# All bias tables first, x loaded after slot 3, DVE's root and scaled tiles before the last four conditioning additions, the sixth conditioning total behind norm 1's sums

## The chip, the cores and the metric

The kernel runs on one core of one Trainium2 chip. The metric is the device time of that core in microseconds (us). The trace is one profiled execution. Engines: PE (TensorE), ACT (ScalarE), DVE (VectorE), POOL (GpSimd), SP (SyncE, which here only issues loads).

## What is computed

Two transformer blocks on x of 256 tokens by 1024, then a norm. What the change touches is the first block's entrance and its second norm:

```python
cond = jax.nn.silu(c)
mod = (cond @ w_ada[l] + b_ada[l]).reshape(b, 6, d)
shift1, scale1, gate1, shift2, scale2, gate2 = [mod[:, i] for i in range(6)]
hn = modulate(rmsnorm(x, norm1_g[l]), shift1, scale1)     # modulate: h * (1 + scale) + shift
proj = hn @ w_in[l]                                       # w_qi is one part of w_in
ya = dsa_attention(..., rel_bias)                         # adds rel_bias by distance of query and key
...
x = x + gate1[:, None, :] * (merged @ w_out[l])           # w_out is w_o in the kernel
hn2 = modulate(rmsnorm(x, norm2_g[l]), shift2, scale2)
f = peer_ffn(hn2, peer_wq[l], ...)                        # w_pq in the kernel
```

## The kernel before

x stands transposed in xT (128 rows by 8 tiles of 256 tokens). Every weight comes as tiles of 128 by 1024 floats (512 KB), in one fixed order (`stream_plan`): 16 tiles of the conditioning weights w_ada, then w_qi (4), w_ki, w_wi, w_qb and so on. Between later tiles the other 32 of w_ada are strewn. Each tile has a slot; the first weights use seven in turn, slots 0 to 3 in `ringb` and 4 to 6 in `far`. SP issues the loads in this order, and waits before each until the slot's last tile has been used up. ACT turns a weight tile into its rounded high part (L1266), DVE (L1794) or POOL (L2574) computes the low part, and PE multiplies with three matmuls for each product (`mm3`).

Conditioning tiles go another way: DVE multiplies each with a column of cond = silu(c) and adds it to `ada_acc` (`ada_add`, L1828 for the first of eight, L1831 for the others). After eight of them PE sums over the rows with eight matmuls of one column (`ada_total`; the trace counts 16, as each float matmul goes in two passes), and DVE adds b_ada (`mod_part`, L1810). The six parts come in the order scale1, shift1, gate1, shift2, scale2, gate2; part g is finished when `mod_done` is g. The scale of part 1 stays in a PSUM bank and goes into the column sm[:, 24:32] (L1996, L1998).

Each engine has a program of its own, written out in order, and waits on semaphores only where it says so. There is no planner; the order in the code is the order of execution. The first stretch:

- ACT: loads vecs, oh and rel_bias, makes cond, waits for slot 5's first tile, issues the loads of cst (identity and ones) and xT, loads the table of the root (L1424), copies bias tables 0 to 3 from PSUM to `sg` (L1428), squares the eight tiles of xT (L1315, with rows of rT used in turn, so that the fifth square waits for the first sum), does the root (L1346), copies bias tables 4 to 7, and then the high parts of the first weights (`splits`).
- PE: bias tables 0 to 3 (`bias_tables`: one matmul of 32 rows and 384 columns for each head, once POOL has spread rel_bias, L2611), sums the squares (`sum_up`, eight matmuls), the first conditioning total, bias tables 4 to 7, the second total, and then the matmuls of w_qi on H.
- DVE: additions of all 16 tiles, the root's correction (L1858 to L1862), the scale column, the eight scaled tiles of x (`scaled`, L1974), mod part 2, and the low parts of H (L2005), each after ACT's high part (L1356).
- POOL: the eight replications, the low parts of w_qi's first two tiles, and then the transfers of the bias tables through DRAM that skew them by rows (L2618, L2623). Before these it waits for the landing of w_qi's fourth tile.

Around the second norm (norm 1 in the code): PE does w_pb, w_pa, the sixth total, w_o, and then the sums of norm 1's squares (`total(1)`). DVE merges the branches in `w_pa`'s loop (L2119 to L2123, the last of which is the low part of H), does mod part 6, waits for mod_done 6, makes the scale column for norm 1 (L2126, L2128), and adds w_o's results to xT (L1904), with low parts of the weights between.

Of the kernel before, what the change touches and what calls it, by code (L numbers as in the profile page):

```python
# [73 lines left out]
def flat(ap):  # L74
    return ap.rearrange("p a b -> p (a b)")
# [226 lines left out]
def square_row(q, k):  # L302

    return ROW[k % 4] if q in (0, 3) or k == 0 else (3, 4, 0)[(k - 1) % 3]


def adds_before(q):
    return sum(ADDS[:q])
# [6 lines left out]
def scaled_before(q):  # L315

    return q - (q > 4)
# [38 lines left out]
def build(nc, A, out, scratch, x_kept):  # L356
    with ExitStack() as ctx:
        V, S, G, TE, SP = nc.vector, nc.scalar, nc.gpsimd, nc.tensor, nc.sync
        P = stream_plan()
# [7 lines left out]
        def sem(name):  # L367
            return ctx.enter_context(nc.semaphore(name))
# [114 lines left out]
        def vec(name, j, n=1):  # L483
            o = VO[name] + j
            return vecs[:, o:o + n]


        slot_in = [sem(f"slot_in{i}") for i in range(13)]
# [6 lines left out]
        cond_done, ada_done, ada_sum, mod_done, mod_prep = (sem(n) for n in ("cond_done", "ada_done", "ada_sum", "mod_done", "mod_prep"))  # L495
# [34 lines left out]
        def ada_bank(g):  # L530

            return 3 if g == 1 else 6
# [17 lines left out]
        def recip(q):  # L550

            return banks[2][:, T:2 * T] if q == 3 else rT[:, 0, :] if q == 4 else banks[7][:, T:2 * T]
# [39 lines left out]
        def tensor_program(t):  # L592
# [4 lines left out]
            def mm(o, l, r, start, stop):  # L597
                return TE.matmul(o, l, r, start=start, stop=stop, skip_group_check=True)  # L598
# [6 lines left out]
            def claim(b):  # L605
                if freed[b]:
                    t.wait_ge(*freed[b])
                return banks[b]

            def ada_total():  # L610
                g, pending = divmod(st["ada"], 8)
                if pending or g == st["sum"]:
                    return
                st["sum"] = g
                b = ada_bank(g - 1)
                o = claim(b)
                t.wait_ge(ada_done, 8 * g)
                t.wait_ge(cst_in, 16)
                for j in range(8):
                    last = mm(o[:, j:j + 1], ada_acc[:, (g - 1) % 2, j * 128:(j + 1) * 128], ones[:, 0:1], True, True)  # L620
                last.then_inc(ada_sum, 1)
                freed[b] = (mod_done, g)

            def ada_unit():
                ada_total()
                st["pos"] += 1
                st["ada"] += 1
# [86 lines left out]
            def of(X):  # L714
                return lambda k: (X[:, 0, k, :], X[:, 1, k, :])
# [9 lines left out]
            def sum_up(q, src, first, last):  # L725
                mm(banks[7][:, 0:T], ones, src, first, last).then_inc(sq_sum, 1)

            def total(q):

                claim(7)  # L730
                t.wait_ge(cst_in, 16)
                t.wait_ge(sq_add, adds_before(q) + 5)
                sum_up(q, squares_sum, True, False)
                for k in (6, 7):
                    t.wait_ge(sq_done, 8 * q + k + 1)
                    sum_up(q, rT[:, square_row(q, k), :], False, k == 7)
                freed[7] = (r_done, q + 1) if q in (4, 6) else (n_t, 8 * scaled_before(q) + 8)
# [83 lines left out]
            def bias_tables(heads):  # L821
                for h in heads:
                    o = claim(bias_bank[h])
                    t.wait_ge(oh_in, 16)
                    t.wait_ge(b_rep, h + 1)
                    mm(o[:, 0:384], ohs[:, 512 + 128 * h:640 + 128 * h], ohs[:, 0:384], True, True).then_inc(b_mm, 1)
                    freed[bias_bank[h]] = (b_cp, h + 1)

            bias_tables(range(4))
            claim(7)  # L830
            t.wait_ge(cst_in, 16)
            for k in range(8):
                t.wait_ge(sq_done, k + 1)
                sum_up(0, rT[:, square_row(0, k), :], k == 0, k == 7)
            freed[7] = (n_t, 8)
            for _ in range(8):
                ada_unit()
            ada_total()
            bias_tables(range(4, 8))
            for _ in range(8):  # L840
                ada_unit()
            ada_total()
# [100 lines left out]
            while U[st["pos"]][0] == "w_ada":  # L943
                ada_unit()
            lin("w_pa", 8, of(Ya), lambda k: t.wait_ge(a_yl, k + 1), kt=4)
            ada_total()
            lin("w_o", 8, hk, lambda k: t.wait_ge(mg_lo, k // 2 + 1))
            total(1)


            def key_scores(c):
# [301 lines left out]
        def scalar_program(s):  # L1253
# [79 lines left out]
            def root(q):  # L1333
                if q == 3:
                    s.wait_ge(s2_sum, 8)
                    s.wait_ge(c_eps, 2)
                    S.activation(s2, banks[3][:, 0:T], ACT.Identity, bias=eps2).then_inc(s2_cp, 1)
                    s.wait_ge(r_done, q)
                    s.wait_ge(z_done, 1)
                    S.activation(rT[:, 1, :], mean(q), ACT.Abs_reciprocal_sqrt).then_inc(rt_done, 1)  # L1340
                    return
                s.wait_ge(sq_sum, sums_before(q + 1))
                s.wait_ge(c_eps, 1)
                if q:
                    s.wait_ge(r_done, q)
                S.activation(rT[:, 1, :], mean(q), ACT.Abs_reciprocal_sqrt, bias=eps).then_inc(rt_done, 1)  # L1346
# [70 lines left out]
            S.dma_start(ohs[:, 384:392], A["rel_bias"]).then_inc(rb_in, 16)  # L1417
            s.wait_ge(vecs_in, 16)
            S.activation(cond[:, :], vec("c", 0, 8), ACT.Silu).then_inc(cond_done, 1)
            s.wait_ge(slot_in[P.slot[5]], 16 * P.use[5])  # L1420
            S.dma_start(cst[:, :], A["cst"]).then_inc(cst_in, 16)
            S.dma_start(xT[:, :, :], A["xT"]).then_inc(x_in, 16)
            s.wait_ge(c_eps, 1)
# [1 line left out]
            def bias_tables(heads):  # L1425
                for h in heads:
                    s.wait_ge(b_mm, h + 1)
                    S.copy(sg[:, 384 * h:384 * h + 384], banks[bias_bank[h]][:, 0:384]).then_inc(b_cp, 1)  # L1428

            bias_tables(range(4))  # L1430
            s.wait_ge(x_in, 16)
            for k in range(8):
                square(0, k, xT[:, k, :])
            root(0)
            bias_tables(range(4, 8))
            for _ in range(16):
                splits()
            s.wait_ge(mod_done, 2)
# [345 lines left out]
        def vector_program(v):  # L1784
# [12 lines left out]
            def lows():  # L1797
                st["pos"] += 1
                lows_until(st["pos"])
# [5 lines left out]
            def mod_part(g):  # L1805
                st["sum"] = g
                o, c = banks[ada_bank(g - 1)], 8 * PARTS[g - 1]
                v.wait_ge(ada_sum, g)
                v.wait_ge(vecs_in, 16)
                V.tensor_tensor(mod[:, c:c + 8], o[:, 0:8], vec("b_ada", c, 8), ALU.add).then_inc(mod_done, 1)  # L1810

            def ada_total():
                g, pending = divmod(st["ada"], 8)
                if not pending and g != st["sum"]:
                    mod_part(g)

            def ada_add():
                n = st["pos"]
                g, k = divmod(st["ada"], 8)
                st["ada"] += 1  # L1820
                lows()
                acc, w = ada_acc[:, g % 2, :], slots[P.slot[n]]
                v.wait_ge(slot_in[P.slot[n]], 16 * P.use[n])
                if k == 0:
                    v.wait_ge(cond_done, 1)
                    if g >= 2:
                        v.wait_ge(ada_sum, g - 1)
                    V.tensor_scalar(acc, w, cond[:, 0:1], None, ALU.mult).then_inc(ada_done, 1)  # L1828
                else:
                    v.wait_ge(ada_done, P.raw_no[n] - 1)  # L1830
                    V.scalar_tensor_tensor(out=acc, in0=w, scalar=cond[:, k:k + 1], in1=acc, op0=ALU.mult, op1=ALU.add).then_inc(ada_done, 1)  # L1831

            def ada_unit():
                ada_total()
                ada_add()
# [46 lines left out]
            def norm(*a, **k):  # L1882
                for _ in norm_steps(*a, **k):
                    pass
# [87 lines left out]
            def scaled(tiles):  # L1972
                for j in tiles:
                    V.scalar_tensor_tensor(out=xs3[:, j, :], in0=xT[:, j, :], scalar=sm[:, 24 + j:25 + j], in1=recip(0),  # L1974
                                           op0=ALU.mult, op1=ALU.mult).then_inc(n_t, 1)
# [10 lines left out]
            V.scalar_tensor_tensor(out=gfm, in0=vec("final_g", 0, 8), scalar=-2.0, in1=vec("norm_mix_g", 0, 8), op0=ALU.mult, op1=ALU.mult).then_inc(c_half, 1)  # L1986
            b1 = vec("b_ada", 8, 8)
            V.tensor_scalar(b1, b1, 1.0, None, ALU.add).then_inc(mod_prep, 1)
            for _ in range(1, 16):
                ada_add()  # L1990
            root(0)

# [5 lines left out]
            V.tensor_tensor(sm[:, 24:32], o[:, 8:16], vec("norm1_g", 0, 8), ALU.mult).then_inc(mod_done, 1)  # L1998
            v.wait_ge(mod_done, 1)
            scaled(range(8))  # L2000
            mod_part(2)
            v.wait_ge(mod_done, 2)
            for j in range(8):
# [111 lines left out]
            for c in range(4):  # L2115
# [5 lines left out]
                V.tensor_tensor(g, g, gb, ALU.add).then_inc(mg_sum, 1)  # L2121
                v.wait_ge(mg_hi, c + 1)
                V.tensor_tensor(flat(H[:, 1, 2 * c:2 * c + 2, :]), g, flat(H[:, 0, 2 * c:2 * c + 2, :]).bitcast(F32), ALU.subtract).then_inc(mg_lo, 1)  # L2123
            ada_total()
            v.wait_ge(mod_done, 6)
            V.tensor_scalar(sm[:, 32:40], mod[:, 32:40], 1.0, None, ALU.add).then_inc(mod_prep, 1)  # L2126
            v.wait_ge(mod_prep, 3)
            V.tensor_tensor(sm[:, 24:32], sm[:, 32:40], vec("norm2_g", 0, 8), ALU.mult).then_inc(mod_prep, 1)  # L2128
# [5 lines left out]
            lows_ahead()  # L2134
            root(1)
            norm(1, xT, lambda j: sm[:, 24 + j:25 + j], shift=lambda j: mod[:, 24 + j:25 + j])


            rc = Tally(rt_c)
# [745 lines left out]
```

## Time and profile before

| | us |
|---|---|
| median of 3 runs | 1471.38 |
| lowest and highest | 1466.09 and 1472.44 |
| the profiled execution | 1468.36 |
| its span, first to last instruction | 1466.6 |
| PE busy | 1408.1 (96%) |
| DVE busy | 1090.3 (74%) |
| ACT busy | 839.3 (57%) |
| POOL busy | 352.3 (24%) |

The profile's page gives busy times, the chain of work that ended last, and the costliest groups of instructions. The trace answers further questions: instructions in order of time, waits, issued loads with their time to landing, the granted clock of TensorE in a stretch. A row of the instructions in order of time has its start, its length, engine and line, operation, what it writes and reads, the count merged into it, and in brackets the idle time before it and what ended that.

### The profile page before, as it was taken

Reading aid. Unit: us, or ns where it says so; the run is one execution under the profiler, and the core shown is the slowest. Engines: PE = TensorE matmul, PEld = TensorE weight load, DVE = VectorE, ACT = ScalarE, POOL = GpSimd, SP = SyncE. Lnnn points to the kernel's source line nnn. Section 1 sums busy time; section 2 is a strip of 40 time slices with the busy share of each in tenths; the row PEclk is TensorE's granted clock in tenths of the full one; section 3 lists DMA queues with packets and bytes.
Section 4 is the critical chain, followed back from the end, with each engine's and each line's share of the span. In section 5 each row is a group of like instructions: output and inputs, shape, how many; then the busy total and the mean of one; then the engine's idle time right before and its main releaser. Section 6 shows DMA issues by size and latency. Waiting matters only on the chain.

```text
span 1466.6 us, 25905 instructions
## 1 busy us (share of the span) xinstructions
PE 1408.1 (96%) x10424; PEld 1310.3 (89%) x10424; DVE 1090.3 (74%) x1905; ACT 839.3 (57%) x1449; POOL 352.3 (24%) x213
## 2 busy tenths in 40 slices
PE   5898999899999999999999999999999999899997
PEld 3887889899999999999988888887889899799997
DVE  6678898666779888899846666677667677888752
ACT  2545684544455677777645454555446666776641
POOL 1322100233445200000023232334322221432300
PEclk9899999999999999999999999999999999999999
DMA  9756766555555644444456666665666535375530
GB/s 374 233 169 211 266 220 224 175 171 164 182 181 167 184 145 146 145 145 149 153 168 219 196 191 194 205 212 179 189 200 248 188 114 187 106 235 186 180 115 30
DMA packets 74009, 269.29 MB, mean 184 GB/s; under 512 B 8433, under 2 KB 9762, under 8 KB 73122
## 3 DMA queue, kind: packets, MB, share of 16 engines
q1 hardware_dynamic: 71568, 257.46, 55.1%
q10 hardware_dynamic: 1426, 7.56, 1.4%
q0 software_dynamic: 896, 2.62, 0.5%
q8 instruction: 83, 1.36, 0.4%
q14 instruction: 36, 0.29, 0.1%
HBM read 263.93 MB, written 3.67 MB: 182 GB/s over the span
## 4 chain that ended last, share of the span: by engine, by line
PE 84%; DVE 9%; ACT 3%; DMA 1%; issue 1%; POOL 1%; SPq 0%; ACTq 0%; DVEq 0%
PE bank L598 83%; DVE split L1794 2%; DVE PR L2238 1%; DVE ada_acc L1831 1%; ACT split L1266 1%; DMA xT<-in_xT 1%; DVE PR L2235 1%; POOL H L2601 1%; DMA far<-in_w_ada 1%; DVE PR L2243 0%; PE bank L771 0%; DVE rT L1874 0%; DVE H L2329 0%; DVE MH L1890 0%; DVE xT L1902 0%
## 5 line engine op out<-in xcount | busy, mean ns | idle before, releaser
L598 PE MATMUL bank<-H,split 128*128 128x256 f32 x5976 | 749.3, 285 | 16.8 <-DVE split L1794 6.0
L598 PEld LDWEIGHTS bank<-H,split 128*128 128x128 f32 x5976 | 726.6, 192 | 24.3 <-issue 8.2
L1266 ACT CAST split<-ringb 128x1024 fp32r<-128x1024 f32 x350 | 365.8, 1046 | 277.4 <-PE bank L598 270.2
L598 PE MATMUL bank<-split,H 128*128 128x512 f32 (+1 forms) x1728 | 389.5, 387 | 4.6 <-DVE H L2329 1.8
L1794 DVE TENSOR_TENSOR split<-ringb,split 128x1024 fp32r<-128x1024 f32 x259 | 324.5, 1255 | 85.2 <-ACT split L1266 85.1
L2574 POOL TENSOR_TENSOR split<-ringb,split 128x1024 fp32r<-128x1024 f32 x91 | 227.1, 2496 | 664.2 <-ACT split L1266 664.2
L598 PEld LDWEIGHTS bank<-split,H 128*128 128x128 f32 x1728 | 320.5, 188 | 71.6 <-issue 4.0
L2329 DVE TENSOR_TENSOR H<-PR,H 128x256 fp32r<-128x256 f32 x128 | 133.5, 1045 | 106.6 <-ACT H L1603 106.6
L1794 DVE TENSOR_TENSOR split<-far,split 128x1024 fp32r<-128x1024 f32 x79 | 105.5, 1342 | 43.2 <-ACT split L1266 42.9
L1266 ACT CAST split<-far 128x1024 fp32r<-128x1024 f32 x91 | 95.0, 1047 | 58.0 <-PE bank L598 53.4
L1579 ACT ACTIVATE PR<-bank 128x512 f32<-128x512 f32 (+31 forms) x59 | 28.6, 486 | 77.9 <-PE bank L598 77.9
L2588 POOL TENSOR_TENSOR rT<-rT 128x256 f32<-128x256 f32 x25 | 25.6, 1025 | 180.5 <-ACT rT L1315 178.8
L598 PE MATMUL bank<-act_t,split 128*128 128x256 f32 x528 | 62.0, 280 | 0.0
L598 PEld LDWEIGHTS bank<-act_t,split 128*128 128x128 f32 x528 | 61.9, 190 | 0.0
L1562 ACT ACTIVATE xT<-cst,rT 128x128 bf16<-128x128 f32 x168 | 55.6, 437 | 0.0
L2300 DVE TENSOR_TENSOR PR<-bank,PR 128x224 f32<-128x224 f32 (+31 forms) x64 | 33.3, 520 | 26.7 <-PE bank L598 26.0
L1603 ACT CAST H<-PR 128x256 fp32r<-128x256 f32 x128 | 51.0, 401 | 0.0
L2290 DVE TENSOR_TENSOR xT<-rt,cpw 128x512 bf16<-128x512 bf16 x126 | 45.7, 418 | 0.0
L2574 POOL TENSOR_TENSOR split<-far,split 128x1024 fp32r<-128x1024 f32 x12 | 29.5, 2456 | 60.3 <-ACT split L1266 60.3
L598 PE MATMUL bank<-Ym,split 128*128 128x256 f32 x336 | 41.5, 282 | 1.5 <-DVE Ym L1949 1.5
L598 PEld LDWEIGHTS bank<-Ym,split 128*128 128x128 f32 x336 | 40.0, 189 | 2.4 <-DVE split L1794 1.7
L598 PE MATMUL bank<-xT 128*128 128x128 bf16 x504 | 36.1, 219 | 0.0
(292 smaller groups left out, 1235.9 us busy)
## 6 DMA issues: line engine op xcount, KB each, us to landing
ringb<-in_u SPq DMA_DIRECT2D x128, 512.0 KB, 3.8
ringb<-in_v SPq DMA_DIRECT2D x128, 512.0 KB, 4.4
ringb<-in_w_ada SPq DMA_DIRECT2D x28, 512.0 KB, 5.4
far<-in_w_up SPq DMA_DIRECT2D x27, 512.0 KB, 4.3
far<-in_w_ada SPq DMA_DIRECT2D x20, 512.0 KB, 5.3
ringb<-in_w_up SPq DMA_DIRECT2D x17, 512.0 KB, 4.7
ringb<-in_w_pq SPq DMA_DIRECT2D x16, 512.0 KB, 3.9
far<-in_w_dn SPq DMA_DIRECT2D x14, 512.0 KB, 3.9
```

The lines of the kernel that those rows point to most:

```text
L598: return TE.matmul(o, l, r, start=start, stop=stop, skip_group_check=True)
L1266: S.copy(buf(m)[0], slots[P.slot[m]]).then_inc(hi_done, 1)
L1562: S.activation(z[:, i // 2, :, i % 2], iota, ACT.Abs, bias=cpn[:, 4 * g + i:4 * g + i + 1]).then_inc(t_abs, 1)
L1579: ins = S.activation(d[:, :, n:T], o[:, :, n:T], ACT.Gelu)
L1603: S.copy(cf[i % 8][0], P3[:, i, :]).then_inc(c_hi, 1)
L1794: V.tensor_tensor(lo, slots[P.slot[m]], hi.bitcast(F32), ALU.subtract).then_inc(lo_v, 1)
L1831: V.scalar_tensor_tensor(out=acc, in0=w, scalar=cond[:, k:k + 1], in1=acc, op0=ALU.mult, op1=ALU.add).then_inc(ada_done, 1)
L2290: ins = V.tensor_tensor(t_gate[g % 3][:, z, :, :, :], t_col[g % 2], of_four(gp[:, 2 + z, :], g), ALU.mult)
L2300: V.tensor_tensor(d[:, 0:n, :], o[:, 0:n, :], d[:, 0:n, :], ALU.mult).then_inc(t_out, 1)
L2329: V.tensor_tensor(lo, P3[:, i, :], hi.bitcast(F32), ALU.subtract).then_inc(c_lo, 1)
L2574: G.tensor_tensor(lo, slots[P.slot[m]], hi.bitcast(F32), ALU.subtract).then_inc(lo_g, 1)
L2588: G.tensor_tensor(acc, acc if k > 1 else rT[:, square_row(q, 0), :], rT[:, square_row(q, k), :], ALU.add).then_inc(sq_add, 1)
```

## The change

Four edits:

1. PE and ACT do all eight bias tables at once at the start. On PE the first eight conditioning tiles' total comes next, ahead of the sums of the squares; on ACT the squares and the root follow the eight copies.
2. ACT waits for slot 3's first tile instead of slot 5's before it issues cst and xT.
3. DVE does the root, the scale column and the scaled tiles after twelve additions, and the last four additions after that.
4. The sixth conditioning total moves on PE from ahead of w_o to behind `total(1)`, and its `mod_part` on DVE to behind norm 1. DVE waits for mod_done 5 in place of 6 before it makes norm 1's scale column.

```diff
@@ tensor_program
-            bias_tables(range(4))
+            bias_tables(range(8))
+            for _ in range(8):
+                ada_unit()
+            ada_total()
             claim(7)
             t.wait_ge(cst_in, 16)
             for k in range(8):
                 t.wait_ge(sq_done, k + 1)
                 sum_up(0, rT[:, square_row(0, k), :], k == 0, k == 7)
             freed[7] = (n_t, 8)
-            for _ in range(8):
-                ada_unit()
-            ada_total()
-            bias_tables(range(4, 8))
             for _ in range(8):
                 ada_unit()
             ada_total()
...
-            ada_total()
             lin("w_o", 8, hk, lambda k: t.wait_ge(mg_lo, k // 2 + 1))
             total(1)
+            ada_total()
@@ scalar_program
-            s.wait_ge(slot_in[P.slot[5]], 16 * P.use[5])
+            s.wait_ge(slot_in[P.slot[3]], 16 * P.use[3])
...
-            bias_tables(range(4))
+            bias_tables(range(8))
...
             root(0)
-            bias_tables(range(4, 8))
@@ vector_program
-            for _ in range(1, 16):
+            for _ in range(1, 12):
                 ada_add()
             root(0)
...
             scaled(range(8))
+            for _ in range(12, 16):
+                ada_add()
             mod_part(2)
...
-            ada_total()
-            v.wait_ge(mod_done, 6)
+            v.wait_ge(mod_done, 5)
...
             norm(1, xT, lambda j: sm[:, 24 + j:25 + j], shift=lambda j: mod[:, 24 + j:25 + j])
+            ada_total()
```

## Rows read from the trace of the kernel before

**Rows 1.** The page: its first line, and the chain's shares by engine.

```profile
span 1466.6 us, 25905 instructions
...
PE 84%; DVE 9%; ACT 3%; DMA 1%; issue 1%; POOL 1%; SPq 0%; ACTq 0%; DVEq 0%
```

**Rows 2.** The chain of waits, 0 to 62 us: start, length, what.

```profile
2.19 0.65 SPq L2719
...
3.38 8.21 DMA far<-in_w_ada
...
11.61 0.35 ACTq L1421
...
12.00 9.94 DMA xT<-in_xT
...
22.52 16.16 PE bank L598 x56
...
41.80 19.13 PE bank L598 x144
```

**Rows 3.** Instructions in order of time, DVE, 0 to 45 us.

```profile
21.15 1.28 DVE L1831 SCALAR_TENSOR_TENSOR ada_acc<-ringb,cond,ada_acc 128x1024 f32<-128x1024 f32 x1 [2.27 <-DMA ringb<-in_w_ada]
22.75 4.06 DVE L1831 SCALAR_TENSOR_TENSOR ada_acc<-far,cond,ada_acc 128x1024 f32<-128x1024 f32 x3 [0.31 <-DMA far<-in_w_ada]
26.91 2.67 DVE L1831 SCALAR_TENSOR_TENSOR ada_acc<-ringb,cond,ada_acc 128x1024 f32<-128x1024 f32 x2
29.72 0.43 DVE L1858 SCALAR_TENSOR_TENSOR bank<-bank,rT 128x256 f32<-128x256 f32 x1
...
31.52 3.22 DVE L1974 SCALAR_TENSOR_TENSOR PA<-xT,sm,bank 128x256 f32<-128x256 f32 x8
38.71 0.17 DVE L1810 TENSOR_TENSOR mod<-bank,vecs 128x8 f32<-128x8 f32 x1 [3.96 <-PE bank L598]
```

**Rows 4.** Instructions in order of time, PE, 0 to 42 us.

```profile
8.39 5.46 PE L598 MATMUL bank<-PA 32*128 32x384 f32 x8 [8.39 <-POOL PA L2611]
22.52 6.65 PE L598 MATMUL bank<-rT,cst 128*128 128x256 f32 x16 [8.68 <-ACT rT L1315]
29.01 1.84 PE L598 MATMUL bank<-cst,ada_acc 128*128 128x1 f32 x16
30.78 4.39 PE L598 MATMUL bank<-PA 32*128 32x384 f32 x8
35.10 3.57 PE L598 MATMUL bank<-cst,ada_acc 128*128 128x1 f32 x16
```

**Rows 5.** Loads issued at 2.19, 11.61 and 39.09: size, us from issue to landing.

```profile
ringb<-in_w_ada SPq DMA_DIRECT2D x1, 512.0 KB, 6.8
...
cst<-in_cst ACTq DMA_DIRECT2D x1, 384.0 KB, 6.5
...
ringb<-in_w_qb SPq DMA_DIRECT2D x1, 512.0 KB, 3.7
```

**Rows 6.** Busy time and granted clock (PEclk) in three stretches.

```profile
core 0: us, PE busy (x) PEld busy (x) DVE busy (x) ACT busy (x) POOL busy (x), PEclk, DMA share, GB/s
8.00:12.00 4.00, 3.61 (x6) 2.05 (x7) 3.79 (x3) 0.00 (x0) 4.00 (x6) 1.00 1.02 409
32.00:36.00 4.00, 4.00 (x11) 1.99 (x9) 2.75 (x8) 1.96 (x5) 0.00 (x0) 0.50 1.00 400
45.00:46.00 1.00, 1.00 (x8) 1.00 (x8) 1.00 (x2) 0.00 (x0) 0.77 (x2) 0.71 1.03 407
```

**Rows 7.** Instructions in order of time, 35 to 42 us: ACT and POOL.

```profile
35.58 1.99 ACT L1266 CAST split<-ringb 128x1024 fp32r<-128x1024 f32 x2
...
36.71 4.66 POOL L2574 TENSOR_TENSOR split<-ringb,split 128x1024 fp32r<-128x1024 f32 x2 [22.85 <-ACT split L1266]
```

**Rows 8.** Instructions on mod: length in ns, least, median and most; first and last start.

```profile
L2005 DVE SCALAR_TENSOR_TENSOR H<-PA,mod,H x8: 467/469/2129, 39.5 to 44.0; 128x256 fp32r<-128x256 f32 x8
```

**Rows 9.** Instructions in order of time, 240 to 290 us: PE and DVE.

```profile
246.88 1.84 PE L598 MATMUL bank<-cst,ada_acc 128*128 128x1 f32 x16
...
250.95 2.36 DVE L1794 TENSOR_TENSOR split<-far,split 128x1024 fp32r<-128x1024 f32 x2
...
252.23 20.42 PE L598 MATMUL bank<-H,split 128*128 128x256 f32 x168 [0.53 <-DVE split L1794]
...
279.00 11.17 PE L598 MATMUL bank<-H,split 128*128 128x256 f32 x71 [3.75 <-DVE H L1878]
```

## The prediction, made before the change was run

> **What bounds the kernel now.** The page first: PE carries 84% of the chain that ended last [rows 1], so an edit pays only where PE stands still or works on something that could be elsewhere. Both places that the change touches are such: the first 42 us, before the dense matmuls on H begin at 41.80, and the stretch around w_o before the second norm. Second view, the chain of waits at the start: the chain runs through the landing of the sixth conditioning tile (3.38 + 8.21 = 11.59), the issue of xT at 12.00, its landing at 21.94, then 16.2 us of PE, mod, and the first H [rows 2]. So before, x is late because ACT waits for slot 5 ahead of issuing cst and xT. Third view, the instructions in order of time, engine by engine: DVE sums conditioning tiles as they land (it waits 2.27 and 0.31 us for landings, then runs without a gap to 29.58), does the root at 29.72, the eight scaled tiles to 34.74, and then waits 3.96 us for PE [rows 3]. PE does the sums of squares at 22.52, the first conditioning total at 29.01, four bias tables at 30.78 and the second total at 35.10 [rows 4]. That is the stretch that the change rearranges: PE's bias tables stand between DVE's last addition (29.58) and the second total (35.10).
>
> **x sooner.** cst is issued when slot 3 has landed instead of slot 5. Slot 3's tile is issued at 2.19 [rows 2] and lands 6.8 us later, at 9.0 [rows 5]; slot 5's landed at 11.59 [rows 2]. The gain is 2.56 us, if the queues share as they do now: cst lands at 15.6 instead of 18.1 (11.61 + 6.5 [rows 2, 5]), xT at 19.4 instead of 21.94. The same 1.4 MB now go ahead of tiles 7 and 8 of the conditioning weights instead of 9 and 10. The queue serves in order, so tile 11 lands at 22.7 as before, and DVE ends its twelfth addition (tile 11) at 22.75 + 1.33 = 24.1, as before [rows 3].
>
> **Bias tables first.** Four tables take PE 5.46 us from 8.39, for one 1.28 us (5.46 for eight matmuls less the last one's drain of 0.2 and the first's delay of 0.1: 0.64 each) [rows 4]. Eight end their issue at 8.39 + the first's extra 0.13 + 8 x 1.28 = 18.8. ACT's copies and GpSimd's eight replications lie inside that. Then PE does the first conditioning total, now ahead of the sums. It takes 1.84 us where the granted clock is full and 3.57 us at half (rows 29.01 and 35.10 [rows 4]; the clock reads 0.50 over the second [rows 6]). Which applies? The clock column reads 1.00 at 8 to 12 [rows 6], yet a bias matmul takes 0.64 us there, twice the 0.32 us that 384 columns in two passes need at 2.4 GHz, and the four at 30.78 begin faster and end at the slow pace once the clock is 0.50. So I take the column as not filled in that early and the level as 1.2 GHz. With it the total ends at 18.8 + 16 x 0.213 = 22.2, and PE, not x, starts the sums: at 22.2 against 22.52. Of the 2.56 us of x, 0.3 are left. If the continuous bias stretch does lift the clock the sums start at 19.4 + 0.6 = 20.0 (0.58 us from landing to the first sum, [rows 2, 4]). I take 22.2, since 3.6 us of bias matmuls out of 4 did not lift it before.
>
> **Root and scaled tiles between the weights.** DVE's wait for the root's table value on ACT now stands after the twelfth addition, with four additions queued behind it. From the first sum to the root is 29.72 - 22.52 = 7.2 us, from there to the end of the scaled tiles 34.74 - 29.72 = 5.02 [rows 3, 4]. So: root at 22.2 + 7.2 = 29.4, scaled tiles done at 34.4. DVE idles from 24.1 to 29.4, while the last four tiles land (the last addition ran at 28.3 before, so its tile was there). Only then come the four additions: 2.67 / 2 = 1.335 each, 5.35 together [rows 3], to 39.8. Before, the last addition ended at 29.58. The second total then costs 3.61 us from its start to mod (35.10 to 38.71) [rows 3, 4], PE having idled since 29: 43.4 without contention.
>
> **GpSimd's lows.** ACT's casts of w_qi stood behind the last bias copies and began at 35.58, GpSimd's two lows at 36.71, 4.66 us for two [rows 7]. With no bias copies behind the root the casts start when ACT has done the root, about 29.5, and the lows run from 30.6 to 35.3. Two effects. The first H low of DVE, which took 2129 ns against a median of 469 [rows 8] while a GpSimd low ran to 41.37, is free: PE starts 1.42 us behind mod (0.81 to the first low, 0.47, 0.14) instead of 41.80 - 38.71 = 3.09, a gain of 1.67. And the additions, which also read two SBUF operands, begin at 34.4, when the second GpSimd low has 0.9 us to go; that costs 0 to 0.9 us, and I take 0.5. The Trainium skill says of this (SBUF - State Buffer, two separate sides) that a VectorE instruction with two SBUF inputs and a GpSimd one that reads SBUF hold the shared port pair in turn, whoever starts first for the whole instruction. The trace agrees in the 2129 ns row; by the rule the delay is the full 0.9, and the sum would be 0.4 higher. It speaks against the change, in that freeing GpSimd's lows moves them onto the additions.
>
> Sum for the start: mod at 39.8 + 0.5 + 3.6 = 43.9 against 38.71, PE's first matmul on H at 45.3 against 41.80: **+3.5 us**. Between 24.1 and 29.4 the idle engine is DVE, and nothing later takes it back, as PE is dense from there (144 matmuls without a gap [rows 2]). What else is queued: SP's loads of w_qi 3, w_ki, w_wi and w_qb 0 wait for additions 12 to 15 and are issued some 8 to 11 us later, w_qi 3 at 35.7. A load in an empty queue lands in 3.7 us [rows 5], so at 39.4; PE wants its cast and low some 9 us after its start, at 54. GpSimd's skew transfers wait for that same landing, and start at 39.4 instead of 41.3. Nothing there. The clock was half until 45.6 before, about 3.8 us into the dense work [rows 6]; the same distance is taken again, with 0 to 1.7 us more if it rises later.
>
> **The last part behind norm 1.** The sixth total (1.84 us on PE at 246.88) leaves the place ahead of w_o. But w_o does not gain that: its first unit needs all H lows, and its second waits for DVE's low, which began at 250.95 and let PE go at 252.23, after 0.53 us of waiting [rows 9]. DVE loses one instruction of 0.17 us there, with 0.02 between. So PE gains **0.2 us** (bounds: 0 and 1.8). Its new place, behind the last sum of norm 1, is inside the 3.75 us that PE waits for H before 279.00 [rows 9]: 1.84 us there cost nothing; if that cover were gone, 1.84. DVE's part of it comes after norm 1 and is one 0.17 us instruction.
>
> Together +3.5 - 0.2 = +3.3 us. The profiled execution took 1468.36 us (span 1466.6), so by it 1471.7; the three runs' median is 1471.38, 3.0 above that execution, which would give 1474.7. I forecast between them: **1473 us**.
>
> **Rivals.** (A) The forecast: PE's order holds the sums until 22.2, the additions come last, +3.3. Chance 0.50.
> (B) The bias stretch lifts the clock to full. Sums at 20.0, root at 27.2, scaled tiles done at 32.2, additions to 37.6, plus up to 2.3 for GpSimd's low that has just begun (lows from 30.4, as the w_qi tiles land at 29.1 and 30.4): mod at 41.2 to 43.5, H at 42.6 to 44.9, +0.8 to +3.1, less 0.2. About 1471. Chance 0.22.
> (C) The trade works: faster. Clock full from early on through the first total and the sums, which then follow ACT's squares: the sums begin at 19.4 to 20 and take half as long, the root falls at 24.1, right behind the twelfth addition, and the additions end at 24.1 + 5.0 + 5.35 = 34.4; mod 1.9 to 3.6 later, at 36.3 to 38, H at 37.7 to 39.4, and w_o pays up to 1.7: -2.6 to -5.8, about 1466. The sums' 6.65 us for 16 matmuls speak against it. Chance 0.15.
> (D) Slower beyond the forecast: the late issues of SP. If w_qi 3 to w_qb 0, and all loads behind them in SP's order, arrive later than PE asks, it stands after its first units, and the clock falls to half again: 4 us of waiting, 1.9 us for the clock (half of 3.8 us), on top of +3.5: +9.4, about 1481. It decides from a landing of w_qi 3 later than about 50 us; I have it at 39.4. Chance 0.06.
> (E) The change does not do what it says: x lands where it did (21.94), since tiles 7 and 8 and cst share otherwise. Then the sums start at 22.5 and all is 0.3 later than in A: 1473.5. Chance 0.07.
>
> **How the numbers follow.** A and E with the open 1.7 us of the clock and both baselines (1468.36 and 1471.38) span 1471 to 1477; B and half of C take the low end to 1467; D is left out but for its near end. Range 1467 to 1479. A measurement of this kernel tells about 0.5% (7.4 us) from no change. None of A, B, C and E comes to that, C only with a low run: faster 0.03. D, and A with a high run: slower 0.08. Same 0.89.
>
> **What would show it.** xT lands near 19.4 (x sooner) or 21.9 (E). PE's first total before its sums; sums from 22.2 (A) or 20.0 (B). DVE idle of 3 to 5 us before L1858's row, L1831's last addition ending at 39 to 41 where it was 29.58. The first mod of the page at 42 to 44, the first L2005 at 0.47 us. PE's wait for w_o's second unit near 1.5 us instead of 0.53. I am wrong if the root comes before 25, or if SP's w_qi 3 lands behind PE's call.

## The result, and the profile after

| | us |
|---|---|
| before, median of 12 runs | 1467.56 |
| changed, median of 12 runs | 1473.74 |
| ratio of the runs | 1.0038, 95% interval 1.0026 to 1.0049 |
| profiled execution, before and changed | 1468.36 and 1471.66 |
| their spans | 1466.6 and 1469.9 |

The changed kernel is 0.38% slower, 5.6 us (3.8 to 7.2) by the ratio. That is clear of the runs' own scatter and below the 0.5% named in the prediction. The two profiled executions differ by 3.3 us, and both differences have to be explained: the 3.3 by the trace, and the other 2 to 3 by something that one pair of executions does not show. (One run of the w_o experiment below, in the slow state, took 2787.65 us and is left out of its ratio. The three runs shown before the prediction had a median of 1471.38; nine more brought it to 1467.56.)

The chain of waits at the start of the changed kernel, with start, length and what; it answers to [rows 2].

```profile
8.38 19.07 PE bank L598 x48
...
33.02 3.01 DVE ada_acc L1829
...
40.23 3.59 PE bank L598 x16
...
45.28 16.72 PE bank L598 x124
```

xT is gone from the chain. In its place the chain runs through 19 us of PE from the first bias table on, and then through DVE's additions (L1829 here, L1831 before) into the second total. The matmuls on H begin at 45.28 against 41.80: 3.48 us later.

DVE in order of time, 22 to 48 us, the lines that answer to [rows 3]:

```profile
22.96 1.28 DVE L1829 SCALAR_TENSOR_TENSOR ada_acc<-far,cond,ada_acc 128x1024 f32<-128x1024 f32 x1
27.98 0.43 DVE L1856 SCALAR_TENSOR_TENSOR bank<-bank,rT 128x256 f32<-128x256 f32 x1 [3.73 <-ACT rT L1345]
...
29.79 3.22 DVE L1972 SCALAR_TENSOR_TENSOR PA<-xT,sm,bank 128x256 f32<-128x256 f32 x8
32.93 4.48 DVE L1829 SCALAR_TENSOR_TENSOR ada_acc<-far,cond,ada_acc 128x1024 f32<-128x1024 f32 x2
37.51 2.67 DVE L1829 SCALAR_TENSOR_TENSOR ada_acc<-ringb,cond,ada_acc 128x1024 f32<-128x1024 f32 x2
43.84 0.17 DVE L1808 TENSOR_TENSOR mod<-bank,vecs 128x8 f32<-128x8 f32 x1 [3.66 <-PE bank L598]
```

DVE waits idle for 3.73 us with four additions queued behind the root, and only then does the root, the scaled tiles and the additions. Two of the additions take 4.48 us where the other two take 2.67: the first was held up, for 1.8 us.

PE in order of time, 0 to 62 us, and GpSimd, 28 to 45 us; these answer to [rows 4] and [rows 7].

```profile
8.38 10.57 PE L598 MATMUL bank<-PA 32*128 32x384 f32 x16 [8.38 <-POOL PA L2611]
18.89 3.57 PE L598 MATMUL bank<-cst,ada_acc 128*128 128x1 f32 x16
22.32 5.11 PE L598 MATMUL bank<-rT,cst 128*128 128x256 f32 x16
40.23 3.57 PE L598 MATMUL bank<-cst,ada_acc 128*128 128x1 f32 x16 [12.80 <-DVE ada_acc L1829]
45.28 16.96 PE L598 MATMUL bank<-H,split 128*128 128x256 f32 x126 [1.48 <-DVE H L2005]
...
30.27 4.66 POOL L2574 TENSOR_TENSOR split<-ringb,split 128x1024 fp32r<-128x1024 f32 x2 [16.42 <-ACT split L1265]
```

The first total stands between the bias tables and the sums without a gap, at the pace of the lower clock level, 1.2 GHz (3.57 us). PE then waits 12.80 us for DVE's last addition.

### The profile page after: what moved, and what is told of

It is laid out like the page before. It is cut to its first block, busy times and chain, and to the rows that moved or that the text cites. A ratio compares the mean times of both kernels' runs of the same rounds, so it can differ in the third digit from the quotient of the medians.

```text
span 1469.9 us, 25905 instructions
## 1 busy us (share of the span) xinstructions
PE 1409.6 (96%) x10424; PEld 1312.1 (89%) x10424; DVE 1091.0 (74%) x1905; ACT 839.6 (57%) x1449; POOL 352.4 (24%) x213
## 3 DMA queue, kind: packets, MB, share of 16 engines
q0 software_dynamic: 896, 2.62, 0.5%
## 4 chain that ended last, share of the span: by engine, by line
PE 85%; DVE 10%; ACT 3%; issue 1%; POOL 1%; DMA 0%; ACTq 0%; DVEq 0%
PE bank L598 84%; DVE split L1792 2%; DVE ada_acc L1829 1%; DVE PR L2238 1%; ACT split L1265 1%; DVE PR L2235 1%; POOL H L2601 1%; DVE PR L2243 0%; PE bank L771 0%; DMA PA<-in_rel_bias 0%; DVE H L2329 0%; DVE MH L1888 0%; DVE rT L1872 0%; DVE PA L1972 0%; DVE xT L1900 0%
```

## The experiments

Each is one edit of the changed kernel or of the kernel before. "H starts" is short for the start of PE's first matmul on H.

**All 16 additions before the root (adds16).** The order of the other edits stays.

```diff
-            for _ in range(1, 12):
+            for _ in range(1, 16):
                 ada_add()
             root(0)
...
             scaled(range(8))
-            for _ in range(12, 16):
-                ada_add()
```

> The changed kernel, with one thing undone: DVE makes all 16 additions before the root and the scaled tiles. Theory 1 (the four additions behind the root set the second total): the last addition ends near 29.6 instead of 40.2, PE's second total runs beside the root and the scaled tiles, DVE is free at 34.7, mod is there at 34.9 and PE's first matmul on H at 36.3 instead of 45.3. That is 9.0 us less than the changed kernel and 5.5 us less than the kernel before: ratio to before 0.996. Rival (the new order on PE, the bias tables in one stretch or GpSimd's lows cost the time, wherever the additions are): H starts after 42, and the time stays within 1 us of the changed kernel.

Measured: median 1464.27 us against 1467.29 of before, ratio 0.9976 (0.9962 to 0.9990); span 1460.6. PE, 0 to 40 us, and two rows of DVE, 28 to 38 us:

```profile
22.07 5.63 PE L598 MATMUL bank<-rT,cst 128*128 128x256 f32 x16
29.80 1.95 PE L598 MATMUL bank<-cst,ada_acc 128*128 128x1 f32 x16 [2.10 <-DVE ada_acc L1829]
36.05 4.21 PE L598 MATMUL bank<-H,split 128*128 128x256 f32 x20 [4.30 <-DVE H L2003]
...
31.47 3.22 DVE L1972 SCALAR_TENSOR_TENSOR PA<-xT,sm,bank 128x256 f32<-128x256 f32 x8
34.61 0.16 DVE L1808 TENSOR_TENSOR mod<-bank,vecs 128x8 f32<-128x8 f32 x1
```

The second total runs beside DVE's root and scaled tiles, H starts at 36.05, 9.23 us before the changed kernel's 45.28, and the medians differ by 9.47. The rival falls: the bias tables in one stretch, x sooner and the w_o part are all still in this kernel, and it beats both others. The place of four additions alone costs the change 9 us: 7.3 for the additions behind the scaled tiles (32.93 to 40.23), 3.6 for the second total and mod, which now stand behind them and not beside DVE's other work, less 1.7 by which root and scaled tiles come sooner. Against the kernel before, the gain is 3.5 us (1.5 to 5.6) and not the 5.5 expected. That 5.5 was counted from the one trace with H at 41.80, and the further traces of the kernel before, below, have it as early as 39.1.

**14 additions before the root (adds14).**

```diff
-            for _ in range(1, 12):
+            for _ in range(1, 14):
...
-            for _ in range(12, 16):
+            for _ in range(14, 16):
```

> The changed kernel with 14 additions before the root and 2 behind the scaled tiles (12 and 4 there). Theory 1, by its price for each addition: 2 x 1.335 us come off DVE's work behind the root, while the two fit into the time in which DVE waits for the root: second total at 37.5 instead of 40.2, H at 42.6 instead of 45.3, 2.7 us less than the changed kernel, ratio to before about 1.001. Rival (only the stall of one addition behind GpSimd's low costs, 1.7 us, and it stays): no gain, H at 45.

Measured: 1470.50 us, ratio to before 1.0019 (1.0007 to 1.0030). DVE and PE, 26 to 43 us:

```profile
27.80 0.43 DVE L1856 SCALAR_TENSOR_TENSOR bank<-bank,rT 128x256 f32<-128x256 f32 x1 [0.79 <-ACT rT L1345]
...
32.75 4.62 DVE L1829 SCALAR_TENSOR_TENSOR ada_acc<-ringb,cond,ada_acc 128x1024 f32<-128x1024 f32 x2
...
37.43 3.58 PE L598 MATMUL bank<-cst,ada_acc 128*128 128x1 f32 x16 [10.18 <-DVE ada_acc L1829]
42.48 0.76 PE L598 MATMUL bank<-H,split 128*128 128x256 f32 x2 [1.48 <-DVE H L2005]
```

H at 42.48, 2.80 us sooner than in the changed kernel (expected 2.7); medians 3.2 apart. Two more additions fill DVE's wait (3.73 becomes 0.79), and each taken from behind the root is worth its own length (2.80 for two of 1.335). The one that is held up stays: 4.62 us for two.

**The w_o part alone, in the kernel before (wo_only).**

```diff
-            ada_total()
             lin("w_o", 8, hk, lambda k: t.wait_ge(mg_lo, k // 2 + 1))
             total(1)
+            ada_total()
...
-            ada_total()
-            v.wait_ge(mod_done, 6)
+            v.wait_ge(mod_done, 5)
...
             norm(1, xT, lambda j: sm[:, 24 + j:25 + j], shift=lambda j: mod[:, 24 + j:25 + j])
+            ada_total()
```

> The kernel before with the w_o part of the change alone (sixth total behind norm 1's sums, mod_done 5 instead of 6). Theory 1: PE is released by DVE's low of w_o's second unit, so only DVE's one instruction counts: 0.1 to 0.2 us less than before, not to be told from no change. Rival A: PE's 1.84 us come off in full, ratio 0.9988. Rival B: the total in the gap of norm 1 delays the matmuls on w_pq or the clock, up to 1.8 us more, ratio 1.0012.

Measured: ratio 1.0001 (0.9987 to 1.0014). PE, 236 to 252 us:

```profile
241.96 3.09 PE L598 MATMUL bank<-Ya,split 128*128 128x256 f32 x24 [1.86 <-DVE split L1794]
245.80 2.41 PE L598 MATMUL bank<-H,split 128*128 128x256 f32 x18 [0.75 <-DVE split L1794]
248.51 0.98 PE L598 MATMUL bank<-H,split 128*128 128x256 f32 x6 [0.30 <-DVE H L2123]
250.06 2.17 PE L598 MATMUL bank<-H,split 128*128 128x256 f32 x16 [0.57 <-DVE split L1794]
```

The 1.84 us of the total come back as three waits for DVE, 0.75, 0.30 and 0.57, where there was one of 0.53 [rows 9]. From the first matmul on H to w_o's second unit it is 250.06 - 39.76 = 210.30 us; before it was 252.23 - 41.80 = 210.43. The gain is 0.13 us. (The other three traces of the kernel before, below, have 210.45, 210.67 and 210.64, so it is 0.1 to 0.4.) The timed runs don't tell that from nothing, and their interval also allows the full 1.84 us (0.9988); it is the trace that excludes it.

**GpSimd's two lows on DVE (lows_dve).**

```diff
         if QI0 <= i < QI0 + 2:
-            return True
+            return False
```

> The changed kernel with the low parts of w_qi's first two tiles on DVE instead of GpSimd. Theory (GpSimd's second low holds up the first of the four additions by 1.7 us): the four additions then take 4 x 1.335 = 5.3 us after the scaled tiles instead of 7.3, the second total starts at 38.4 instead of 40.2. PE's first matmul on H is later all the same, near 47.5, since DVE now makes the low part of the first weight tile behind the eight lows of H. Rival (the first addition is slow for another reason, such as the wait on its landing): second total at 40.2 again.

Measured, one execution: 1476.40 us. DVE, 30 to 50 us, and PE, 37 to 50 us:

```profile
33.43 2.67 DVE L1829 SCALAR_TENSOR_TENSOR ada_acc<-far,cond,ada_acc 128x1024 f32<-128x1024 f32 x2
36.20 2.67 DVE L1829 SCALAR_TENSOR_TENSOR ada_acc<-ringb,cond,ada_acc 128x1024 f32<-128x1024 f32 x2
...
38.93 3.57 PE L598 MATMUL bank<-cst,ada_acc 128*128 128x1 f32 x16 [10.99 <-DVE ada_acc L1829]
47.79 2.57 PE L598 MATMUL bank<-H,split 128*128 128x256 f32 x8 [5.29 <-DVE split L1792]
```

With GpSimd idle the pair takes 2.67 us instead of 4.48, and from the first of the four additions to the second total it is 5.50 us instead of 7.30. So 1.80 us of the changed kernel's start are the wait for GpSimd's second low. As a version it loses: H starts at 47.79, as PE waits 5.29 us for the low part that DVE now makes.

**cst and xT after slot 5 again (x_late).** One line: slot and use 5 instead of 3 in ACT's wait.

> The changed kernel with cst and xT issued after slot 5's landing, as before. Theory (PE's first total, not x, sets the first sum): xT lands near 22.0, the sums start at 22.5 instead of 22.3, H within 0.4 us of the changed kernel's 45.3. Rival (x sooner is worth its 2.3 us of landing): H at 47.5.

Measured, one execution: 1473.30 us. PE, 0 to 46 us.

```profile
18.71 3.57 PE L598 MATMUL bank<-cst,ada_acc 128*128 128x1 f32 x16
22.23 5.78 PE L598 MATMUL bank<-rT,cst 128*128 128x256 f32 x16
...
45.19 1.19 PE L598 MATMUL bank<-H,split 128*128 128x256 f32 x4 [1.48 <-DVE H L2005]
```

xT landed at 21.7 instead of 19.65, and H started at 45.19 instead of 45.28. The sums follow PE's first total in both (22.23 and 22.32). In this order the earlier x is worth nothing.

**The sums ahead of the first total (sums_first).**

```diff
             bias_tables(range(8))
-            for _ in range(8):
-                ada_unit()
-            ada_total()
             claim(7)
...
             freed[7] = (n_t, 8)
+            for _ in range(8):
+                ada_unit()
+            ada_total()
```

> The changed kernel with PE's first conditioning total behind the sums of the squares instead of ahead of them. By my steps: the sums start 0.6 us behind x, at 20.2 instead of 22.3, and end 2 us sooner; the total behind them, at 27, takes 1.84 to 3.57 us, and DVE's scale column waits for it until 28.9 to 30.6 (29.4 in the changed kernel). The additions still begin while GpSimd's lows run, so H comes between 44.3 and 45.5. Rival (the sums' start is what holds the chain): H 2.1 us sooner, at 43.2.

Measured, one execution: 1473.49 us. DVE, 22 to 44 us, then GpSimd and PE.

```profile
26.13 0.43 DVE L1856 SCALAR_TENSOR_TENSOR bank<-bank,rT 128x256 f32<-128x256 f32 x1 [1.88 <-ACT rT L1345]
...
31.08 5.90 DVE L1829 SCALAR_TENSOR_TENSOR ada_acc<-far,cond,ada_acc 128x1024 f32<-128x1024 f32 x2
...
30.27 5.63 POOL L2574 TENSOR_TENSOR split<-ringb,split 128x1024 fp32r<-128x1024 f32 x2 [16.40 <-ACT split L1265]
...
44.87 1.41 PE L598 MATMUL bank<-H,split 128*128 128x256 f32 x5 [1.48 <-DVE H L2005]
```

Here the earlier x was used (sums at 20.27, root 1.85 us sooner), and 0.4 us arrived at H. Both additions were held up this time, 2.6 and 3.2 us long, and GpSimd's two lows took 5.63 instead of 4.66. I had put this down to the total behind the sums; it took 1.84 us and held nothing. The interval was met, by the other of its two terms: an addition that begins earlier only meets more of GpSimd's work.

**More traces of the two kernels, unchanged.**

> The kernel before, once more with a profile, to see how its start varies. The runs' medians lie 6 us apart where the two profiled executions lie 3.3 apart. Theory 2: where the granted clock rises and falls differs between executions (it rose at 28.5 and fell at 31.9 in the first profile of before), and the kernel before can gain from it in its second group of bias tables and second total (4.39 and 3.57 us at half), the changed one cannot, since its second total always follows a long idle stretch. Then PE's first matmul on H moves between about 39.5 and 42 here. Rival: the start is the same to 0.2 us and the difference arises elsewhere.

> The changed kernel once more with a profile. Theory 2 (its start does not gain or lose where the clock changes elsewhere, since the first addition is held until GpSimd's low ends at 34.9 and the second total follows an idle stretch): H at 45.3 to 45.9 and the second total 3.57 us, whatever the place of the clock's steps; the runs differ by what comes after. Rival: H moves by over 1 us, as it did between the first looks at the kernel before (41.8) and at the w_o part alone (39.8).

> The kernel before, a third look. Theory 2, after the looks so far (its start code gave H at 41.80 and 41.86 where the clock fell at 32.0, and at 39.76 in the w_o part alone, where it fell at 33.5; the changed kernel's H stayed at 45.3 at either): where the clock's first fall comes later than 32.5, GpSimd's lows and the second total come sooner and H is at 39.5 to 41; where it falls at 32.0 again, H is at 41.8 again. Rival: H is at 41.8 wherever the clock falls, and the w_o look was another thing.

> The kernel before, a fourth look, with the same expectations as the third: H between 39.5 and 41 where the clock falls after 32.5, 41.8 where it falls at 32.0; the span 1463 to 1465 in the first case and 1466.6 in the second. Rival: 41.8 in both.

Measured, the kernel before: 1468.46, 1468.45 and 1466.38 us, with spans of 1466.7, 1466.7 and 1464.6. The second trace repeated the first (H at 41.86). The third and the fourth did not. PE of the fourth, 22 to 42 us, and its busy time and granted clock in one stretch, columns as in [rows 6]:

```profile
27.85 1.84 PE L598 MATMUL bank<-cst,ada_acc 128*128 128x1 f32 x16
29.62 2.84 PE L598 MATMUL bank<-PA 32*128 32x384 f32 x8
32.40 2.98 PE L598 MATMUL bank<-cst,ada_acc 128*128 128x1 f32 x16
39.09 3.12 PE L598 MATMUL bank<-H,split 128*128 128x256 f32 x13 [3.71 <-DVE H L2005]
...
33.00:34.00 1.00, 1.00 (x8) 1.00 (x7) 1.00 (x3) 1.00 (x2) 0.00 (x0) 0.54 1.04 414
```

and two lines of the third:

```profile
33.19 2.92 PE L598 MATMUL bank<-cst,ada_acc 128*128 128x1 f32 x16
39.88 2.48 PE L598 MATMUL bank<-H,split 128*128 128x256 f32 x10 [3.77 <-DVE H L2005]
```

The second group of bias tables takes 2.84 us instead of 4.39 and the second total 2.98 and 2.92 instead of 3.57. The granted clock fell in the middle of the total (33.1 in the fourth trace, 33.9 in the third) and not at 32.0, in the middle of the tables. ACT's copies and GpSimd's lows follow: the lows end at 38.67 and 39.45 (41.37 in the first trace), and each time H starts 0.42 or 0.43 us behind that. DVE's first low of H takes 2.62 and 2.61 us there (2.13 in the first trace [rows 8], 0.47 by itself). So in the kernel before PE waits for DVE's first low of H, and that for GpSimd's second low, and H starts there anywhere from 39.1 to 41.9.

Two parts of the expectation were missed. The fourth trace's H is 0.4 us ahead of the stretch given for it, and the third trace, with H 1.92 us sooner than the first, is no shorter: 1466.7 us. Busy time and clock in the third trace, then in the fourth:

```profile
754.00:758.00 4.00, 3.90 (x10) 3.16 (x11) 2.52 (x5) 1.37 (x3) 0.00 (x0) 0.57 0.46 135
...
754.00:758.00 4.00, 4.00 (x19) 3.30 (x18) 1.95 (x4) 1.88 (x4) 0.00 (x0) 1.00 0.44 133
```

In the third trace, and in the w_o trace, the clock fell once more around 754 us, for 3.4 us. In the other three traces of the kernel before it did not. An earlier H is thus not yet a shorter execution.

The changed kernel's second trace (1473.59 us) gave H at 45.27, as the first (45.28), and yet a span of 1471.8 instead of 1469.9. Busy time and granted clock in three stretches, columns as in [rows 6], second trace:

```profile
49.00:50.00 1.00, 1.00 (x7) 1.00 (x6) 1.00 (x2) 0.00 (x0) 0.00 (x0) 0.50 1.05 409
50.00:51.00 1.00, 1.00 (x10) 1.00 (x10) 0.16 (x1) 0.00 (x0) 0.00 (x0) 0.96 1.00 392
...
248.00:251.00 3.00, 3.00 (x15) 3.00 (x16) 2.28 (x4) 1.56 (x2) 0.00 (x0) 0.51 0.64 213
```

and in the first:

```profile
49.00:50.00 1.00, 1.00 (x10) 1.00 (x9) 1.00 (x2) 0.00 (x0) 0.00 (x0) 0.95 1.01 399
...
248.00:251.00 3.00, 2.57 (x22) 2.37 (x21) 2.28 (x4) 1.57 (x2) 0.00 (x0) 1.00 0.62 178
```

The clock rose 1 us later behind the start of the dense matmuls, and fell once more at 248. In the four traces of the kernel before, the rise came 3.8, 3.8, 4.3 and 4.2 us behind H, and there was no fall around 245. In the changed kernel H is tied to the additions, and the clock rose 3.8 and 4.8 us behind it. The H of the kernel before moves with the place where the clock falls.

## Why the prediction was right, and where it was not

**x sooner.** Predicted landing 19.4, measured 19.65; tile 11's addition ended at 24.2 (24.1). Right, and so was that PE and not x starts the sums (22.2 forecast, 22.32 measured); x_late shows the worth of it as nothing.

**Bias tables first.** Right: 1.2 GHz throughout the tables, total from 18.89 at 3.57 us. Rivals B and C, which let the bias matmuls lift the clock, are out.

**From the sums to the root.** 7.2 us were taken from the first profile of before; 5.66 were measured (6.15 in the second trace). By the pace of the matmuls the clock rose near 25.2 and not near 28.5; the clock column reads 1.00 throughout there and does not show it. The root came at 27.98 instead of 29.4. A term mis-sized by 1.5 us.

**GpSimd's lows.** That they move onto the additions was forecast, for 0.5 us with bounds of 0 and 0.9. It was 1.80: because the root came early, the first addition began (32.93) just behind the start of the second low (32.6) and lasted 3.09 us instead of 1.285. The low ended at 34.93, the addition at 36.02, nearly its own length later. By the Trainium skill's rule (SBUF - State Buffer, two separate sides) whoever starts first keeps the port for the whole instruction, and the trace agrees, here and in lows_dve and sums_first. The two misses are linked and cancel: the additions ended at 40.18 against 40.3 forecast. So it is in the second trace, where the root came 0.5 us later, the first addition took 2.58 us, and H began at the same time. An earlier root brings little: 1.85 us at the root gave 0.41 at H in sums_first. That the forecast of H is right to 0.1 us is in this part luck.

**The rest of the start.** L2005 at 480 ns each without the 2129 ns one, and H 1.44 us behind mod (1.42). Mod at 43.84 (43.9), H at 45.28 (45.3). SP's w_qi 3 landed near 41 instead of 39.4. Only GpSimd's skew transfers waited for it, and they began at 41.19, as before (41.31): rival D is out. Rival E, x landing as before, is out.

**w_o.** 0.2 forecast, 0.13 measured in the w_o trace and in the changed kernel's first: 255.58 - 45.28 is again 210.30. The sign named for it, a wait near 1.5 us at w_o's second unit, did not come so: that wait was 0.57, and two others stood ahead of it (0.75 and 0.30), 1.62 together. PE already waited for DVE in the first unit. The total behind norm 1 ran at 278.44 for 1.84 us, under PE's wait for H, which ended 3.36 us later than before (282.36 against 279.00), the start's 3.48 less 0.12.

**The size.** Against the profiled execution the sum was +3.3 and the spans say +3.3. Against the runs it was too small: 5.6 (3.8 to 7.2). The step that was off is the first one, taking one execution of the kernel before as the kernel: its H at 41.80 and its clock. That H was at the late end: 39.1 and 39.9 in two other traces, 39.8 in the w_o trace, whose start is the same. I had allowed 0 to 1.7 us for the clock after H and nothing for its effect ahead of H. The time of 1473.74 lies on the forecast of 1473 by luck, for two reasons that cancel: the base of 1468.36 to 1471.38 was up to 4 us too high, the step too small by 2. The range (1467 to 1479) held either way.

How much of the missing 2.3 us is H and how much the clock behind it is not settled: four traces of one kernel and two of the other are too few for a mean, and the third shows that the clock can take back what an early H gives. The timed runs suggest that the clock has a part. Their mean granted clock over the whole execution is 0.987 in the changed kernel (12 runs) and 0.990 in the kernel before (the 29 runs beside the experiments). Where both read 0.988, two runs each, they took 1473.1 and 1473.8 against 1470.5 and 1470.8 us: 2.8 apart and not 5.6. Why the changed kernel's runs have the lower clock no run here shows.

## What to carry to other kernels

Before moving work between the pieces of a sum, ask when the last piece arrives and what already runs beside the total. Filler belongs in an idle stretch of its engine, and here the root's inputs came 3.7 us after that stretch had begun. The root and the scaled tiles, put ahead of the additions, delayed the one result that everything waited for, while in the other order the same work runs beside PE's total. Take the start of a kernel from more than one trace before a sum of a few us is made against it, and compare the clock of the executions along with their times.

## What the runs showed of the hardware

The granted clock reads 1.00 in the first 25 us although the matmuls run at the pace of half: 16 bias matmuls in 10.57 us there, 8 in 2.84 us at the full clock in the fourth trace of before, 0.66 against 0.36 us each. A column of ones is no safe reading ahead of the first step that the trace holds.

A total of eight matmuls of one column on fresh weights (16 in the trace) took 3.57 us at the low level and 1.84 at the high one, and in three traces the clock fell in the middle of such a total (33.1, 33.5 and 33.9) though PE was busy. A VectorE addition of two SBUF operands, 1.28 us by itself, took up to 3.2 us beside GpSimd's low (2.3 us), and GpSimd's pair of lows grew from 4.66 to 5.63; the scaled tiles, which read one operand from PSUM, kept their 3.22 us beside the same low.
